# Expert stages of a two-layer encoder: from gathered rows to all experts computed densely

## What is computed

```python
q = (x @ w_q).reshape(B, S, PEER_HEADS, 2, PEER_DK // 2)
s = jnp.einsum('bshcd,cnd->bshcn', q, sub_keys)      # 8 heads, 2 halves, 128 keys
sv, si = lax.top_k(s, PEER_TOPK)                     # 16 best of each half
cand_s = sv[..., 0, :, None] + sv[..., 1, None, :]   # 256 pairs
best_s, pos = lax.top_k(cand_s, PEER_TOPK)           # 16 best pairs = experts
e_idx = jnp.take_along_axis(cand_i, pos, axis=-1)    # expert = key1 * 128 + key2
gate = jax.nn.softmax(best_s, axis=-1)
hid = jax.nn.gelu(jnp.einsum('td,ted->te', xt, u[et]), approximate=False)
y = jnp.einsum('te,ted->td', gt * hid, v[et])
```

## Time and profile before

| what | value |
|---|---|
| median of 3 runs, not profiled | 1824.02 us (1819.15 to 1825.95) |
| span of the profiled execution | 1995.1 us |
| PE busy | 1482.2 us, 74% |
| DVE busy | 1007.4 us, 50% |
| POOL busy | 1016.4 us, 51% |
| ACT busy | 342.9 us, 17% |
| read from memory | 590.37 MB |

### The profile page before, as it was taken

How to read it: one execution, slowest core, us unless ns; L and a number is a source line. 1 busy time by engine, 2 the same in 40 slices (tenths; PEclk the granted TensorE clock), 3 DMA queues, 4 the chain that set the end, 5 groups by cost and what they waited for, 6 DMA issues and landing times.

```text
span 1995.1 us, 18642 instructions
## 1 busy us (share of the span) xinstructions
PE 1482.2 (74%) x4236; PEld 720.2 (36%) x4236; DVE 1007.4 (50%) x2400; ACT 342.9 (17%) x921; POOL 1016.4 (51%) x1197
## 2 busy tenths in 40 slices
PE   7997467777666877766889974577776777777677
PEld 5775233344322422222345552244432222222223
DVE  0226766666664544444122267666666645434442
ACT  1222111111111111111123221111110211111111
POOL 1111556655566466666400005555555666666663
PEclk8998688888898989999988887988888999998999
DMA  7764998999899799999812228989997999999996
GB/s 167 153 142 158 327 372 328 331 340 331 329 356 371 281 358 367 375 366 369 300 49 57 54 78 323 352 323 342 336 337 303 364 371 378 362 359 365 361 372 259
DMA packets 236447, 591.86 MB, mean 297 GB/s; under 512 B 59136, under 2 KB 100736, under 8 KB 236416
## 3 DMA queue, kind: packets, MB, share of 16 engines
q0 software_dynamic: 147456, 536.94, 71.5%
q1 hardware_dynamic: 88960, 54.57, 10.5%
HBM read 590.37 MB, written 1.05 MB: 296 GB/s over the span
## 4 chain that ended last, share of the span: by engine, by line
PE 22%; DVE 22%; issue 19%; POOL 13%; DMA 9%; another core or an unknown queue 5%; DVEq 3%; ACT 2%; POOLq 2%; SPq 1%; ACTq 1%
DVE u_rows L1124 9%; POOL v_rows L446 6%; POOL u_rows L439 6%; PE att L671 6%; DMA v_rows<-in_peer_v_dram,idx_v 5%; PE y L554 3%; DMA u_rows<-in_peer_u_dram,idx_u 3%; PE b_qk L565 3%; PE b_vo L574 1%; ACT shared L924 1%; PE att L527 1%; PE att L524 1%; DVE hit L1094 1%; DVE hit L1090 1%
## 5 line engine op out<-in xcount | busy, mean ns | idle before, releaser
L1124 DVE CUSTOM_DVE_ANT_0 u_rows<-y,u_rows 128x1024 f32<-128x1024 f32 x512 | 615.4, 1222 | 460.0 <-DMA u_rows<-in_peer_u_dram,idx_u 412.9
L446 POOL DMA_INDIRECT v_rows<-in_peer_v_dram,idx_v x512 | 483.8, 945 | 319.6 <-issue 147.0
L671 PE MATMUL att<-v_rows,shared 128*128 128x512 f32 x1024 | 510.8, 631 | 172.9 <-DMA v_rows<-in_peer_v_dram,idx_v 131.4
L439 POOL DMA_INDIRECT u_rows<-in_peer_u_dram,idx_u x512 | 485.6, 948 | 240.2 <-issue 158.6
L671 PE MATMUL y<-v_rows,shared 128*128 128x512 f32 x1024 | 493.1, 630 | 81.4 <-DMA v_rows<-in_peer_v_dram,idx_v 52.6
L671 PEld LDWEIGHTS att<-v_rows,shared 128*128 128x128 f32 x1024 | 184.3, 196 | 498.7 <-issue 454.3
L671 PEld LDWEIGHTS y<-v_rows,shared 128*128 128x128 f32 x1024 | 197.4, 202 | 368.3 <-issue 360.0
L646 PE MATMUL b_vo<-keysT,qT 128*128 128x128 f32 x128 | 28.4, 359 | 199.6 <-ACT qT L908 136.1
L924 ACT ACTIVATE shared<-ident,wts 128x128 f32<-128x128 f32 x512 | 154.2, 387 | 65.7 <-PE att L671 38.3
L919 ACT ACTIVATE act_hid<-hid 128x16 f32<-128x16 f32 x32 | 6.9, 216 | 819.9 <-issue 446.2
L632 PE MATMUL b_qk<-hT,w_pq 128*128 128x256 f32 x448 | 103.8, 392 | 3.8 <-DMA w_pq<-in_peer_w_q_dram 3.8
(11 more groups left out here) (158 smaller groups left out, 1068.1 us busy)
## 6 DMA issues: line engine op xcount, KB each, us to landing
w_pq<-in_peer_w_q_dram SPq DMA_DIRECT2D x16, 1024.0 KB
w_qk<-in_na_w_in_dram SPq DMA_DIRECT2D x16, 512.0 KB, 5.0
u_rows<-in_peer_u_dram,idx_u POOLq DMA_INDIRECT x512
v_rows<-in_peer_v_dram,idx_v POOLq DMA_INDIRECT x512
w_v<-in_na_w_in_dram SPq DMA_DIRECT2D x8, 512.0 KB, 3.8
shared<-in_na_rel_bias_dram SPq DMA_DIRECT2D x64, 64.0 KB, 4.6
w_o<-in_na_w_out_dram SPq DMA_DIRECT2D x8, 512.0 KB, 4.0
w_o<-in_mla_w_out_dram SPq DMA_DIRECT2D x8, 512.0 KB, 3.4
```

What stands on the lines that cost most here:

```text
L439: pool.indirect_dma_start(u_rows[:, b, :], None, u_table, bass.IndirectOffsetOnAxis(ap=idx_u[:, half_no, b:b + 1], axis=0))\
L446: pool.indirect_dma_start(v_rows[:, b, :], None, v_table, bass.IndirectOffsetOnAxis(ap=idx_v[:, half_no, b:b + 1], axis=0))\
L671: last = nc.tensor.matmul(ffn[tile][:, c, :], diag[:, k, :], v_rows[:, b, c * 512:(c + 1) * 512], start=False, stop=stop and k == TOPK - 1)
L1124: V.tensor_tensor_reduce(out=rows, in0=px, in1=rows, scale=1.0, scalar=0.0, op0=ALU.mult, op1=ALU.add, accum_out=hid[:, k:k + 1])\
```

## The change

Both tables are read whole, once per layer and in order, by plain DMAs on the SP queue. On the host `peer_u` is laid out so that item `j` (j is the second key, 0 to 127) holds the 128 experts of all first keys as a 128x1024 block that can serve as the stationary operand; `peer_v` likewise by `j`, and the query weights in the same size. All items pass through one ring of 7 buffers of 512 KB (`stream`, 272 items per layer: 16 of query weights, 128 of `u`, 128 of `v`).

PE computes the inner product of every expert with every token: for item `j`, 8 matmuls over the width with 256 moving columns (`hidden_pair` does two items). ACT applies Gelu and stores into `H` (128 first keys x 128 items x 256 tokens, 128 KB per partition). The choice becomes gates: for each token, DVE makes two one-hot matrices from the 128 choices (`one_hots`: first key with the gate as value, second key), PE multiplies them (`gate_chunk`, 8 tokens at a time, 16 chunks per tile) and so has the 128x128 gates of that token in PSUM. DVE multiplies them into `H` (`weigh_chunk`): where the inner values are there already (`DONE`), it multiplies; into the others it copies the gate, and multiplies later with the values that ACT kept in `held` (`weigh_held`). Then PE multiplies `H` with the `v` items (`add_experts`, 4 matmuls of 512 columns per item).

Attention's buffers now lie inside `H`. POOL has no work in the expert stage. The choice itself (`choose`, `finish_choice`) does the old steps, with the last part done for all 8 heads of a tile at once. Tile 0's final norm no longer comes halfway: both tiles end together, except that the last 6 `v` items are done first for tile 0 and then for tile 1 (`TAIL_V`), and the latents of both tiles come after.

```diff
-CHOICES = PH + 2
-RING = 8
 NEG = -1e30
+
+RING = 7
+HALF = 2 * PH + KEYS
+ITEMS = HALF + KEYS
+NPAIRS = KEYS // 2
+CHUNK = 8
+CHUNKS = P // CHUNK
+SG = 11
+T0_PAIR = 16
+T1_PAIR = NPAIRS - SG
+DONE = (2 * T0_PAIR, 2 * T1_PAIR)
+SPARE = 16 - SG
+TAIL_V = RING - 1
...
+        H = sb("H", [P, KEYS, TOK])
...
+            def stream(item, src):
+                if item >= RING:
+                    sp.wait_ge(s_item, item - RING + 1)
+                sp.dma_start(ring[:, item % RING, :], src).then_inc(s_land[item % RING], 16)
...
+            def stream_pair(layer, m):
+                for j in (2 * m, 2 * m + 1):
+                    stream(u_item(layer, j), peer_u[layer, j])
...
+            stream_u(0)
+            stream_v(0, range(80))
...
-                    for b in range(RING):
-                        k = half_no * RING + b
...
-                            pool.wait_ge(s_acc, products_done(base + (g - 1) * TOPK + k + 1 - RING))
-                            pool.sem_inc(s_pool, 1)
-                            pool.indirect_dma_start(v_rows[:, b, :], None, v_table,
-                                                    bass.IndirectOffsetOnAxis(ap=idx_v[:, half_no, b:b + 1], axis=0))\
-                                .then_inc(s_vg[b], 16)
...
+            def hidden_pair(layer, m):
+                if m >= 2:
+                    pe.wait_ge(s_hid, layer * NPAIRS + m - 1)
+                for e in range(2):
+                    w = stream_wait(u_item(layer, 2 * m + e)).rearrange("p (k i) -> p k i", k=DK)
...
+                        last = nc.tensor.matmul(hid_ps[m % 2][:, e, :], w[:, k, :], hT[:, k, :],
+                                                start=(k == 0), stop=(k == DK - 1))
+                    last.then_inc(s_item, 1)
...
+            def gate_chunk(layer, t, c):
+                n = chunk_no(layer, t, c)
+                pe.wait_ge(s_hot, n + 1)
+                if t or c >= 2:
+                    pe.wait_ge(s_gw, n - 1)
+                for s in range(CHUNK):
+                    last = nc.tensor.matmul(G_ps[n % 2][:, s, :], A_hot[n % 2][:, s, :], B_hot[n % 2][:, s, :],
+                                            start=True, stop=True)
+                last.then_inc(s_gps, 1)
+
+            def gated_pairs(layer, t, first):
+                choice_transposes(layer, t)
+                for m in range(first, first + SG):
+                    hidden_pair(layer, m)
+                    for c in chunks_behind(m, first):
+                        gate_chunk(layer, t, c)
+
+            def add_experts(layer, t, j, rows):
...
+                    last = nc.tensor.matmul(ffn[t][:, c, :], H[:, j, t * P:(t + 1) * P], rows[:, c * 512:(c + 1) * 512],
+                                            start=False, stop=(j == KEYS - 1))
...
-            def add_experts(layer, tile, g, stop=False):
-
-                base = layer * GROUPS
-                for k in range(TOPK):
-                    b = k % RING
-                    pe.wait_ge(s_diag, (base + g) * TOPK + k + 1)
-                    pe.wait_ge(s_vg[b], 16 * ((base + g) * 2 + k // RING + 1))
-                    for c in range(2):
-                        last = nc.tensor.matmul(ffn[tile][:, c, :], diag[:, k, :],
-                                                v_rows[:, b, c * 512:(c + 1) * 512],
-                                                start=False, stop=stop and k == TOPK - 1)
...
+                peer_queries(layer, 0)
+                for h in range(1, PH):
+                    peer_queries(layer, h)
+                    key_scores(layer, h - 1)
+                    hidden_pair(layer, h - 1)
+                key_scores(layer, PH - 1)
+                for m in range(PH - 1, T0_PAIR):
+                    hidden_pair(layer, m)
+                gated_pairs(layer, 0, T0_PAIR)
+                for m in range(T0_PAIR + SG, T1_PAIR):
+                    hidden_pair(layer, m)
+                gated_pairs(layer, 1, T1_PAIR)
...
+                for j in range(KEYS - TAIL_V):
+                    if j == DONE[1]:
+                        pe.wait_ge(s_held0, held_before(layer, NPAIRS))
+                        pe.wait_ge(s_held1, (layer + 1) * SG)
+                    rows = stream_wait(v_item(layer, j))
+                    add_experts(layer, 0, j, rows)
+                    add_experts(layer, 1, j, rows).then_inc(s_item, 1)
+                for j in range(KEYS - TAIL_V, KEYS):
+                    last = add_experts(layer, 0, j, stream_wait(v_item(layer, j)))
+                last.then_inc(s_acc, 1)
+                for j in range(KEYS - TAIL_V, KEYS):
+                    add_experts(layer, 1, j, ring[:, v_item(layer, j) % RING, :]).then_inc(s_item, 1)
...
+            for t in range(TILES):
+                norm_transposes(norm_no(0, 1, t), t, ffn_banks[t])
+            for t in range(TILES):
+                latents(t)
+            for t in range(TILES):
+                latents_transposed(t)
...
+            def activate_pair(layer, m):
+                act.wait_ge(s_item, u_item(layer, 2 * m + 1) + 1)
+                pair = H[:, 2 * m:2 * m + 2, :]
+                if m < T0_PAIR:
+                    nc.scalar.activation(pair, hid_ps[m % 2], ACT.Gelu).then_inc(s_hid, 1)
+                    return
+                if m - (SG if m < T1_PAIR else SPARE) >= (T0_PAIR if m < T1_PAIR else T1_PAIR):
+                    act.wait_ge(s_held0, slot0_free(layer, m))
+                nc.scalar.activation(held[:, slot0(m), :, :], hid_ps[m % 2][:, :, 0:P], ACT.Gelu)
+                if m >= T1_PAIR:
+                    act.wait_ge(s_held0, slot1_free(layer, m))
+                    pair1 = held[:, slot1(m), :, :]
+                else:
+                    pair1 = pair[:, :, P:TOK]
+                nc.scalar.activation(pair1, hid_ps[m % 2][:, :, P:TOK], ACT.Gelu).then_inc(s_hid, 1)
...
+            def one_hots(layer, t, c):
+
+                n = chunk_no(layer, t, c)
+                for s in range(CHUNK):
+                    at = c * CHUNK + s
+                    V.tensor_scalar(A_hot[n % 2][:, s, :], iota128[:, :], choice[:, 0, at:at + 1], choice[:, 2, at:at + 1],
+                                    ALU.is_equal, ALU.mult)
+                V.tensor_tensor(B_hot[n % 2], iota128[:, :].unsqueeze(1).broadcast_to([P, CHUNK, KEYS]),
+                                choice[:, 1, c * CHUNK:(c + 1) * CHUNK].unsqueeze(2).broadcast_to([P, CHUNK, KEYS]),
+                                ALU.is_equal).then_inc(s_hot, 1)
+
+            def weigh_chunk(layer, t, c):
+
+                n = chunk_no(layer, t, c)
+                dve.wait_ge(s_gps, n + 1)
+                at = t * P + c * CHUNK
+                done = H[:, 0:DONE[t], at:at + CHUNK]
+                later = H[:, DONE[t]:KEYS, at:at + CHUNK]
+                gates = G_ps[n % 2].rearrange("p t j -> p j t")
+                V.tensor_tensor(done, done, gates[:, 0:DONE[t], :], ALU.mult)
+                V.tensor_copy(later, gates[:, DONE[t]:KEYS, :]).then_inc(s_gw, 1)
...
+                for c in range(CHUNKS):
+                    weigh_chunk(layer, t, c)
+                    if c + 2 < CHUNKS:
+                        one_hots(layer, t, c + 2)
+                    while t == 1 and m < first + c * SG // CHUNKS:
+                        weigh_held(layer, m, 0)
+                        m += 1
...
+                for h in range(PH):
+                    choose(layer, 1, h)
+                    for _ in range(2):
+                        weigh_held(layer, m, 0)
+                        m += 1
...
+    laid['peer_u'] = _np.asarray(inputs['peer_u']).reshape(LAYERS, KEYS, KEYS, DK, P).transpose(0, 2, 4, 3, 1)\
+        .reshape(LAYERS, KEYS, P, D)
+    laid['peer_v'] = _np.asarray(inputs['peer_v']).reshape(LAYERS, KEYS, KEYS, D).transpose(0, 2, 1, 3)
```

More of the change, by code:

```diff
@@ new lines, in program @@
+        best_e = sb("best_e", [P, PH, TOPK])
+        gate_s = sb("gate_s", [P, PH])
+        gate_r = sb("gate_r", [P, PH])
+        gate = sb("gate", [P, PH, TOPK])
+        choice = sb("choice", [P, 3, P])
+        ab = sb("ab", [P, 2, 2, CHUNK, KEYS])
+        A_hot = [ab[:, 0, b, :, :] for b in range(2)]
+        B_hot = [ab[:, 1, b, :, :] for b in range(2)]
+        hit = ab[:, :, :, :, :].rearrange("p x b c n -> p (x b c n)").rearrange("p (h n) -> p h n", n=TOPK)
+        held = sb("held", [P, 16, 2, P])
@@ new lines, in choice_transposes @@
+            def choice_transposes(layer, t):
+                pe.wait_ge(s_chosen, 2 * layer + t + 1)
+                for r, src in enumerate((pick[:, 0, :], pick[:, 1, :], gate[:, :, :].rearrange("p h k -> p (h k)"))):
+                    last = nc.tensor.transpose(choice_ps[:, r, :], src, ident[:, :])
+                last.then_inc(s_chT, 1)
+            def gate_chunk(layer, t, c):
[7 more added lines that the diff above has]
+                last.then_inc(s_gps, 1)
@@ L799, in _ @@
             pe.wait_ge(s_cT, TILES)
+            pe.wait_ge(s_kpsb, TILES)
+            for t in range(TILES):
```

(52 more changed lines are left out.)

642 lines of the change are left out of this document (268 added, 374 removed).

## The result

The changed kernel takes **2405.34 us** (median of 4 runs, 2404.26 to 2405.74), the kernel before 1824.99 us (4 runs, 1819.15 to 1827.5): ratio 1.3199, 95% interval 1.3167 to 1.3231. Forecast were 2410 us, with 0.96 for slower. The profiled execution took 2405.74 us itself; its span is 2403.6.

A forecast was written before the change was run, and what follows sets the result against it. Gather transfers were taken to bound the expert stages and PE the mixers. With PE binding the dense stages, 381 us of surroundings, 2 x 1011 us of PE work and 7 us of handovers gave 2410 us; range 2350 to 2540.

The forecast's parts named there:

- What bounds the kernel before: Expert stages of 821 and 809 us: transfers bound them, DMA engines 91% busy, PE's 590 and 572 us under them.
- Which time the sum is made against: Profiled 1995 against unprofiled 1824 us: the 171 us lie on the gathers, so the sum forecasts unprofiled time too.
- the profiler stretches everything alike: Rival on the whole span: the profiler lengthens all parts in proportion, giving 2203 us; chance 0.04.
- What a matmul costs: PE, float32 at four cycles per column: 0.2356, 0.4325 and 0.8606 us for 128, 256 and 512 columns.
- the estimate of 2010 us: PE's matmuls priced by the skill's sustained stream figures: 812 us per layer, about 2010 us in all, still slower.
- What stays under it: Gates in the expert stages: DVE's chunk takes 4.3 us against PE's 6.6, so PE does not wait.
- The feared price of reading PSUM with a stride: Rival in `weigh_chunk`, DVE binds the gates: at four times the price a chunk takes 8.5 us, 2530 us; chance 0.13.
- The stream: Items take 1.4 to 2.0 us against PE's 3.46, hidden at no cost; rival, not hidden: 2704 us, chance 0.04.
- Surroundings: Outside the expert stages: start 177, handover 36, second mixer 156, end 12, together 381 us.
- The 7 us for handovers: Allowance for each tile's first gate chunks and the handovers: 7 us, a choice, none to 20 possible.
- the clock: Rival in both expert stages: PE's granted clock falls to 0.91, adding 200 us, 2610 us; chance 0.04.
- weight loads alone: Rival on PE in the dense stage: only weight loads count, 692 us a layer, total 1772 us; chance 0.03.

The follow-up runs named there:

- two versions of the changed kernel: Changed kernel with DVE making the one-hot rows B once more per chunk, 2408.55 us; changed kernel with every stream item loaded a second time, 2410.54 us.

## Why the prediction was right

**What bounds the kernel before: right.** Transfers bound the stages: without those of `u` it falls to 1501 us, until PE binds.

**Which time the sum is made against: this step failed.** "So I take the profiler's cost to lie on the gathers" is half wrong. The 171 us do lie in the gather stages (168 by the stretches), and 368 GB/s was near the 378 to 382 measured; but they are no cost of the profiler, which takes at most 0.6%: the profiled execution lasted as long as runs at the slower level do. (The job of that profile isn't on record.) It is luck that the step did no harm to the number: the changed kernel has no gathers, and its terms came from stretches that read alike at both levels. The rival "the profiler stretches everything alike" (2203) rested on the same error. What does depend on it is the verdict's size: 32% slower against 1822 to 1825 us, but 19 to 21% against 1995 to 2019, the changed kernel's 2405 us taken as measured in the other jobs.

**What a matmul costs: right.** 0.432, 0.223 and 0.8583 us (24 records in 10.30 us in the `v` products) against 0.4325, 0.2356 and 0.8606 in the forecast. The term of 128 columns was 5% too high: 288 x 0.0126 = 3.6 us a layer, which with the `v` products' 1.2 us makes the layer's 1011 us into 1006.4 and 1007.7. The Trainium skill (TensorE: Matmul & The Clock Gate, Back-to-back issue gap) has two figures for the distance of matmuls. Its sustained one, 131 ns for 512 columns, which gave the estimate of 2010 us, doesn't hold for these float32 passes: 0.8583 / 4 = 215 ns. Its other one, N / 2.4 + 2.5 ns, which it gives for a single matmul, agrees: four times it is 863 and 223 ns.

**What stays under it: right, with the margins as said.** DVE's chunk was 4.3 us in the forecast and is 4.4 to 4.5: the eight `TENSOR_SCALAR` take 2.13 us, not 1.7, and what they overlap with the others makes up for most of it. One more operation is hidden but for 5.9 us, three are not. The feared price of reading PSUM with a stride did not come: 0.42 us for 256 elements and 0.95 us for 768 are 1.04 ns per element more, the slope of the earlier trace rows. The Trainium skill's rule of the 8-byte lines (SBUF — State Buffer, Door 1) thus shows no price for DVE at these two operations. The stream: hidden, as the doubled transfers show, but the reason given, 1.4 to 2.0 us an item, isn't enough by itself; with a ring of 2 the bandwidth is the same and 125 us are lost. Seven buffers hide it, and five did with twice the bytes; how few would do isn't shown.

**Surroundings: 381 us forecast, 389.5 measured.** Start 177 and end 12 as forecast. The handover took 39.2 us, not 36, the mixer 161.3, not 156. Its granted clock is 0.85, in the earlier trace rows 0.88; 156 x 0.88 / 0.85 is 161.5 us, which fits but was not tried. In the handover the timeline of PE shows the rest:

```profile
1216.58 6.12 PE L522 MATMUL y<-nat,alpha_ident 128*128 128x512 f32 x8 [4.40 <-DVE nat L1056]
1222.63 1.94 PE L776 MATMUL qv<-H 128*64 128x256 f32 x8
```

Four seeds of 512 columns, 3.44 us at 0.86 each, take 6.05 us, at a granted clock of 0.59: 2.6 us more than their price. The wait of 4.40 us before them wasn't in the sum either; the rest of the handover took less than its share of the 36, so that 3.2 us lack in all.

**The 7 us for handovers: too much by 7.** PE waits nowhere inside the stages. Terms: 177 + 1006.4 + 39.2 + 161.3 + 1007.7 + 12 = 2403.6. The errors, -7 -8 +8.5, nearly cancel: that the sum came within 0.2% is luck, that it came within the range is not.

**Rivals.** DVE and the stream bind only in the runs that make them; the clock stayed at 1.00; weight loads alone would have given 1772 and no change with half the columns.

## What to carry to other kernels

Before a gathered stage is made dense, price the matmuls that come new at the pace that the trace shows for their width and type; here the dense `u` products cost 443 us a layer and replaced work that lay under transfers. Saving bytes buys nothing beyond the point where another engine's queue is longer: 269 MB fewer were worth less than 4096 records on PE. Where float32r is good enough for the products, the same dense form is the fastest of the three.

When the profiled time and the timed runs differ, look first whether the same kernel has more than one level, and profile it again, before the profiler is blamed.

## What was not expected of the hardware

- The kernel before has two levels, 1822 and 1995 to 2019 us, by the job, and only with gathers for both tables: with plain transfers for `u` it took 1807 and 1808 us, and two versions of the changed kernel 2409 and 2411 us in jobs of the slower level.
- After a wait of 3.77 us PE's next 3.3 us ran at a granted clock of 0.55. Waits of PE in the gated stretches cost over half more than themselves (83 us of waits, 34 and 12 us of slower clock).
- float32r halves the records per matmul and brings 256 columns from 0.432 to 0.125 us.
- DVE reads PSUM at a stride of 512 bytes at the price of contiguous elements.
